# HGRN key and value transposes moved into the local stage, decayed sample states on ScalarE, products by 32-row groups and read-outs in halves

## What is computed

```python
def step(S, inp):
    qc, kc, vc, lf = inp
    G = jnp.cumsum(lf, axis=2)
    Gl = G[:, :, -1]
    o_inter = jnp.einsum('bhik,bhkv->bhiv', qc * jnp.exp(G), S)
    diff = G[:, :, :, None, :] - G[:, :, None, :, :]
    decay = jnp.exp(jnp.where(mask, diff, -jnp.inf))
    A = jnp.einsum('bhik,bhjk,bhijk->bhij', qc, kc, decay)
    o = o_inter + jnp.einsum('bhij,bhjv->bhiv', A, vc)
    S = S * jnp.exp(Gl)[..., None] + jnp.einsum('bhjk,bhjv->bhkv', kc * jnp.exp(Gl[:, :, None, :] - G)[..., None], vc)
    return S, o
```

## Time and profile before

| | |
|---|---|
| median of three timed runs | 2321.52 us |
| the profiled execution | 2320.4 us |
| its span, first to last instruction | 2318.2 us |
| PE / DVE / ACT / POOL busy | 97% / 65% / 55% / 47% |
| mean granted clock of TensorE | 0.984 |
| local_block, layer 0 and layer 1 | 20.18 and 21.73 us |
| hgrn_block, layer 0 and layer 1 | 42.82 and 45.81 us |

### The profile page before, as it was taken

How to read it: one execution, slowest core, us unless ns; L and a number is a source line. 1 busy time by engine, 2 the same in 40 slices (tenths; PEclk the granted TensorE clock), 3 DMA queues, 4 the chain that set the end, 5 groups by cost and what they waited for, 6 DMA issues and landing times. The chain is left out here.

```text
span 2318.2 us, 58007 instructions
## 1 busy us (share of the span) xinstructions
PE 2247.4 (97%) x20562; PEld 2076.7 (90%) x20562; DVE 1495.5 (65%) x3062; ACT 1267.3 (55%) x2437; POOL 1088.8 (47%) x990
## 2 busy tenths in 40 slices
PE   7999999999999999999989999999999999999998
PEld 4967779999998899999978586899999988999997
DVE  3876339943227878788668663598322296887885
ACT  3652225576558855555556422455855596555554
POOL 0221018864446656566304010498444474665661
PEclk8999999999999999999999889999999999999999
DMA  7472135555553389899454702455555534998982
GB/s 290 155 254 94 65 132 182 180 199 185 187 189 137 109 275 312 274 310 314 163 181 160 277 5 102 155 182 181 199 189 185 189 109 139 310 312 272 308 300 100
DMA packets 123816, 455.53 MB, mean 197 GB/s; under 512 B 13745, under 2 KB 14257, under 8 KB 122545
## 3 DMA queue, kind: packets, MB, share of 16 engines
q1 hardware_dynamic: 105264, 386.80, 46.9%
q0 software_dynamic: 18432, 67.12, 10.6%
HBM read 449.37 MB, written 4.49 MB: 196 GB/s over the span
## 5 line engine op out<-in xcount | busy, mean ns | idle before, releaser
L446 POOL TENSOR_TENSOR parts<-ring,parts 128x512 fp32r<-128x512 f32 x358 | 463.4, 1298 | 469.5 <-ACT parts L439 455.7
L439 ACT ACTIVATE parts<-ring 128x512 fp32r<-128x512 f32 x620 | 389.3, 632 | 352.3 <-PE ps_u L493 281.2
L489 PE MATMUL ps_u<-h_parts,parts 128*128 128x256 f32 x4096 | 563.1, 280 | 0.9 <-ACT parts L439 0.6
L2739 PE MATMUL ps_y<-act_parts,parts 128*128 128x256 f32 x4096 | 563.6, 280 | 0.0
L489 PEld LDWEIGHTS ps_u<-h_parts,parts 128*128 128x128 f32 x4096 | 514.7, 188 | 3.2 <-ACT parts L439 1.9
L2739 PEld LDWEIGHTS ps_y<-act_parts,parts 128*128 128x128 f32 x4096 | 515.8, 188 | 0.8 <-ACT parts L2679 0.7
L446 DVE TENSOR_TENSOR parts<-ring,parts 128x512 fp32r<-128x512 f32 x262 | 187.1, 720 | 360.5 <-ACT parts L439 336.1
L2788 POOL TENSOR_TENSOR act_parts<-big,act_parts 128x256 fp32r<-128x256 f32 x256 | 245.0, 957 | 306.2 <-ACT act_parts L2768 306.2
L493 PE MATMUL ps_u<-h_parts,parts 128*128 128x256 f32 x2048 | 322.2, 279 | 1.2 <-DVE parts L446 0.9
L2743 PE MATMUL ps_y<-act_parts,parts 128*128 128x256 f32 x2048 | 322.5, 279 | 0.0
L493 PEld LDWEIGHTS ps_u<-h_parts,parts 128*128 128x128 f32 x2048 | 275.5, 188 | 2.0 <-DVE parts L446 1.3
(11 more groups left out here) (410 smaller groups left out, 2824.5 us busy)
## 6 DMA issues: line engine op xcount, KB each, us to landing
ring<-in_stream SPq DMA_DIRECT2D x506, 512.0 KB, 3.4
more_ring<-in_stream SPq DMA_DIRECT2D x126, 512.0 KB, 3.5
extra_ring<-in_stream SPq DMA_DIRECT2D x32, 512.0 KB, 5.9
mod_ring<-in_stream SPq DMA_DIRECT2D x32, 512.0 KB, 3.3
big<-in_stream SPq DMA_DIRECT2D x16, 512.0 KB, 11.5
out_state_out<-big SPq DMA_DIRECT2D x2, 1440.0 KB, 8.1
big<-in_state SPq DMA_DIRECT2D x2, 1280.0 KB, 10.8
big<-in_mixc SPq DMA_DIRECT2D x2, 1024.0 KB, 8.3
```

The lines of the kernel that those rows point to most:

```text
L439: eng.activation(m.parts[:, q % PARTS, 0, :], half_tile(m, t, half), ACT.Copy).then_inc(s["hi_ready"], 1)
L446: eng.tensor_tensor(m.parts[:, q % PARTS, 1, :], half_tile(m, t, half), m.parts[:, q % PARTS, 0, :].bitcast(F32), ALU.subtract).then_inc(m ...
L489: pe.matmul(out, hi[:, k, :], hr[:, side, kk, 0:tokens], start=(kk + side == 0), stop=False)
L2739: pe.matmul(ps[:, half * KD // 2 + k, :], hi[:, k, :], act_parts[:, j % AHEAD, side, :], start=False, stop=False)
```

## The change

- `ktt` and `vtok` get a place of their own at the end of the area, and the twelve transposes with their six copies move into `local_block`: PE has them in front of 14 fillers in place of 24, then the tiles 4 to 7, and only then the head spread, which now also waits for the copies (`kt_out`).
- In `hgrn_block` the masked values are stored once per row group: the 128 tokens are four groups of 32 rows, each with four chunks of 8. Four masked copies serve 16 chunks. `products(tt, first, end)` runs matmuls over 32 rows each with 256 columns, one bank of `ps_outer` for each row group: 16 matmuls for the first 16 chunks in one call, and 8 in each of two calls for the other 16.
- The samples' decayed states are 16 ScalarE activations of 64 columns in place of two GpSimd products.
- `read_samples` and `read_states` run in halves between the tiles, `sample_products` one pair at a time; the first tile goes ahead of `distance(0)`, `turn(3)` behind the last read-out, and four fillers end PE's list. ScalarE's last copy of rows moves behind the copy of the prompt's last state.
- DVE takes the states in runs of 16, 8 and 8.

The diff, cut to its core:

```diff
-            keep_busy(pe, m, ps[:, 0, :], 24)
+            for tt, (t0, n) in enumerate(TOK):
+                for pair in range(A_PAIRS):
+                    pe.transpose(ps[0:n, tt, pair * P:(pair + 1) * P], m.kt[:, pair, t0:t0 + n], m.ident)
+                for pair in range(A_PAIRS):
+                    mm = pe.transpose(ps[0:n, tt, (2 + pair) * P:(3 + pair) * P], m.zact[:, 4 + pair, t0:t0 + n], m.ident)
+                mm.then_inc(s["turned"], 1)
+            keep_busy(pe, m, ps[:, 3, :], 14)
+            ada(KD // 2, KD)
             pe.wait_ge(s["qk_inverse"], 1)
+            pe.wait_ge(s["kt_out"], 3)
             for n in range(6):
                 mm = pe.matmul(ps[:, n, 0:NT], m.mix("head_spread")[0:12, n * P:(n + 1) * P], norm, start=True, stop=True)
             mm.then_inc(s["qk_spread"], 1)
-            ada(KD // 2, KD)
             turn(0)
...
+            for tt, (_, n) in enumerate(TOK):
+                act.wait_ge(s["turned"], tt + 1)
+                act.activation(flat(m.ktt[0:n, tt, :, :]), ps[0:n, tt, 0:2 * P], ACT.Copy)
+                act.activation(m.vtok[0:n, tt, :], ps[0:n, tt, 2 * P:4 * P], ACT.Copy).then_inc(s["kt_out"], 1)
...
+            def mask_v(tt):
+
+                values = vtok[:, tt, :].rearrange("p (h v) -> p h v", h=4)
+                for j in range(GROUP):
+                    i = act.activation(vm[:, tt, :, j, :], values, ACT.Copy, scale=m.mix("block_rows")[:, j:j + 1])
                 i.then_inc(s["vm_ready"], 1)
 
...
             mask_v(0)
+            mask_v(1)
             copy_rows(act, m, s, ada_rows, ps_mod, 1)
             copy_columns(act, m, s, ps_mod, 1, 1)
-            mask_v(1)
-            mask_v(2)
-            mask_v(3)
+            mask_samples()
+            for pair in range(A_PAIRS):
+                for b in range(NB):
+                    t = NP + NS * b + NS - 1
+                    i = act.activation(m.states[:, pair, 1 + b, :], m.state0[:, pair, b, :], ACT.Copy,
+                                       scale=since[:, pair, t:t + 1])
+                i.then_inc(s[f"kept{pair}"], 1)
             copy_rows(act, m, s, ada_rows, ps_mod, 2)
             copy_columns(act, m, s, ps_mod, 2, 2)
-            mask_v(4)
-            copy_rows(act, m, s, ada_rows, ps_mod, 3)
-            copy_columns(act, m, s, ps_mod, 3, 3)
             for pair in range(A_PAIRS):
                 act.wait_ge(s[f"after{pair}"], BLOCKS)
             act.activation(m.states[:, 0:A_PAIRS, 0, :], after[:, :, BLOCKS - 1, :], ACT.Copy)
-
-        @block.gpsimd
-        def _(pool):
-            for pair in range(A_PAIRS):
-                last = blocks(since, True, NS - 1, NS)[:, pair, :, :].broadcast_to([P, NB, HD])
-                pool.tensor_tensor(m.states[:, pair, 1:, :], m.state0[:, pair, :, :], last, ALU.mult).then_inc(
-                    s[f"kept{pair}"], 1)
+            copy_rows(act, m, s, ada_rows, ps_mod, 3)
+            copy_columns(act, m, s, ps_mod, 3, 3)
...
+            def products(tt, first, end):
+
+                pe.wait_ge(s["vm_ready"], tt + 1)
                 for pair in range(A_PAIRS):
-                    if step >= 2:
-                        pe.wait_ge(s[f"after{pair}"], HALF * (step - 1))
-                    for r in range(2):
-                        rows = slice(r * HD, (r + 1) * HD)
-                        mm = pe.matmul(ps_outer[rows, (2 * step + pair) % 4, :], ktt[:, step // 2, pair, rows],
-                                       vm[:, step % 2, 2 * pair + r, :, :], start=True, stop=True)
-                    mm.then_inc(s["u_ready"], 1)
-
-                pe.wait_ge(s["vm_ready"], 5)
+                    if tt:
+                        pe.wait_ge(s[f"after{pair}"], GROUP * end)
                 for pair in range(A_PAIRS):
-                    pe.wait_ge(s[f"after{pair}"], HALF * 3)
-                    for r in range(2):
-                        rows = slice(r * HD, (r + 1) * HD)
-                        mm = pe.matmul(ps_outer[rows, pair, :], ktt[0:NB * NS, 2, pair, rows],
-                                       vm[0:NB * NS, 0, 2 * pair + r, :, :], start=True, stop=True)
-                    mm.then_inc(s["samples_u"], 1)
-
-            for tt, (t0, n) in enumerate(TOK):
-                for pair in range(A_PAIRS):
-                    pe.transpose(ps_outer[0:n, tt, pair * P:(pair + 1) * P], kt[:, pair, t0:t0 + n], m.ident)
-                for pair in range(A_PAIRS):
-                    mm = pe.transpose(ps_outer[0:n, tt, (2 + pair) * P:(3 + pair) * P], v[:, pair, t0:t0 + n], m.ident)
-                mm.then_inc(s["turned"], 1)
+                    for group in range(first, end):
+                        tokens = slice(32 * group, 32 * group + 32)
+                        for r in range(2):
+                            rows = slice(r * HD, (r + 1) * HD)
+                            mm = pe.matmul(ps_outer[rows, group, pair * GROUP * HD:(pair + 1) * GROUP * HD],
+                                           ktt[tokens, tt, pair, rows], vm[tokens, tt, 2 * pair + r, :, :], start=True, stop=True)
+                mm.then_inc(s["u_ready"], 1)
+
+            def sample_products(pair):
+
+                pe.wait_ge(s["vm_ready"], 3)
+                for other in range(A_PAIRS):
+                    pe.wait_ge(s[f"after{other}"], TB + GROUP * (pair + 1))
+                for r in range(2):
+                    rows = slice(r * HD, (r + 1) * HD)
+                    mm = pe.matmul(ps_outer[rows, pair, :], ktt[0:NB * NS, 2, pair, rows],
+                                   vms[0:NB * NS, 2 * pair + r, :, :], start=True, stop=True)
+                mm.then_inc(s["samples_u"], 1)
+
+            ada(8, 9)
             distance(0)
-            ada(8, 9)
             distance(1)
             ada(9, 11)
             distance(2)
             ada(11, 12)
             distance(3)
-            ada(12, 14)
+            pe.wait_ge(s["sample_free"], 1)
+            read_samples(0, NB // 2)
             distance(4)
+            ada(12, 13)
+            distance(5)
+            products(0, 0, 4)
+            distance(6)
+            ada(13, 14)
+            distance(7)
             ada(14, 16)
-            distance(5)
-            products(0)
-            distance(6)
+            read_samples(NB // 2, NB).then_inc(s["sample_read"], 1)
             turn(1)
-            distance(7)
-            read_samples()
-            ada(16, 20)
-            products(1)
-            ada(20, 24)
-            products(2)
+            ada(16, 17)
+            pe.wait_ge(s["values_done"], 1)
+            read_states(0, 0)
+            ada(17, 19)
+            products(1, 0, 2)
+            read_states(0, 1)
+            ada(19, 21)
+            read_states(1, 0)
+            ada(21, 22)
+            products(1, 2, 4)
+            ada(22, 24)
+            read_states(1, 1)
             turn(2)
-            pe.wait_ge(s["values_done"], 1)
-            read_states(0)
+            sample_products(0)
             ada(24, 27)
-            products(3)
-            read_states(1)
+            read_states(2, 0)
             ada(27, 29)
-            sample_products()
-            ada(29, 32)
-            read_states(2)
+            read_states(2, 1)
+            ada(29, 30)
+            sample_products(1)
+            ada(30, 32)
+            read_states(3, 0)
+            read_states(3, 1).then_inc(s["inter_ready"], 1)
             turn(3)
-            mm = read_states(3)
-            mm.then_inc(s["inter_ready"], 1)
+            keep_busy(pe, m, ps_outer[:, 3, :], 4)
...
-            for turn in range(4):
-                ve.wait_ge(s["u_ready"], 2 * turn + 2)
-                for b in range(turn * HALF, (turn + 1) * HALF):
+            for first, ready in ((0, 1), (TB, 2), (TB + HALF, 3)):
+                ve.wait_ge(s["u_ready"], ready)
+                for b in range(first, TB if ready == 1 else first + HALF):
                     for pair in range(A_PAIRS):
-                        new, j = after[:, pair, b, :], b % HALF
-                        add = ps_outer[:, (2 * turn + pair) % 4, j * HD:(j + 1) * HD]
+                        new = after[:, pair, b, :]
+                        add = ps_outer[:, b // GROUP % 4, (pair * GROUP + b % GROUP) * HD:(pair * GROUP + b % GROUP + 1) * HD]
```

More of the change, by code:

```diff
@@ L1233, in inter, with read_samples @@
                 return pe.matmul(out[rows], state[rows], qt[rows, pair, t:t + n], start=True, stop=True)
[L1235 to L1238 removed]
+            def read_samples(first, end):
+                for b in range(first, end):
                     for pair in range(A_PAIRS):
```

61 lines of the change are left out of this document (25 added, 36 removed).

## The result

| | before | after |
|---|---|---|
| median of the runs | 2318.81 us (18 runs, 2314.68 to 2324.93) | 2335.82 us (18 runs, 2324.51 to 2347.83) |
| ratio after / before, 95% interval | | 1.0077 [1.0064, 1.0089] |
| profiled execution (span) | 2320.4 (2318.2) us | 2347.8 (2345.8) us |
| mean granted clock of it | 0.984 | 0.968 |
| local_block, layer 0 and 1 | 20.18 and 21.73 us | 26.67 and 22.31 us |

The change makes the kernel 17 us slower. The forecast of 2311.0 and its range up to 2320 were both too low; what came is the mechanism of the fourth rival (2333), to which the prediction gave a chance of 0.04. The profiled execution of after is the longest of its 18, so its stages show the effect large: 30.1 us in the two pairs of stages, where the medians differ by 17.0. Its runs scatter over 23 us, those of before over 10.

What follows compares the result with a forecast made beforehand. TensorE, busy 97% of the span, was taken as the bound. Both layers' -11.0 us at full clock and 4.5 back from layer 1 made -15.5; clock falls added 6.1, so -9.4 from 2320.4 gave 2311.0, range 2303 to 2320.

Steps and rivals of the forecast that it cites:

- the fourth rival: HGRN stage: clock stays at half, its dense work of 22 us per layer doubles; 2333 us, chance 0.04.
- The HGRN stage's sum at full clock: HGRN stage, per layer: seven gains and costs on PE sum to -6.0 us.
- first product: HGRN stage start: DVE's 512-column product falls from 1590 ns to 0.70 us with GpSimd silent; gain 1.6 us.
- `distance(0)` at 1.0: HGRN stage start: `distance(0)` starts 1.0 us after the stage in place of 2.63.
- products near 1.1 per call: HGRN stage: overlapping row groups bring the three products calls from 7.8 us to 3.3 together; gain 4.5 us.
- rivals 2 and 3: HGRN stage: 2, row groups don't overlap, 2320, chance 0.13; 3, slow first product isn't GpSimd's doing, 2314, chance 0.10.
- DMA was put at nothing: HGRN stage: tile loads cost nothing, as each tile has six to eight others ahead of it.
- 0.6 for extra changes of kind: HGRN stage: read-outs in halves add changes between kinds of matmul; cost 0.6 us, bounds 0.3 and 1.2.
- the 0.17 at the end: HGRN stage end: `turn(3)` behind the reads and four filler matmuls; net cost 0.17 us.
- the second half of "The clock": HGRN stage, second samples' reads and `turn(1)`: one fall in the two layers, 3.5 us at half, cost 1.7 us.
- The first half: Change from local to HGRN stage: clock falls in both layers; cost 2.2 us per layer, bounds 0 and 3.4.
- The local stage: Local stage, per layer: transposes and tiles ahead of the head spread cost 0.5 us, bounds 0 and 1.3.

Runs made afterwards that it cites:

- three-filler version: Change with three fillers at nine places, old place of tiles 4 to 7, four fillers behind the head spread, three ahead of `distance(0)`: 2310.31 us, 0.9963 of before.
- whole read-outs: Changed kernel with halves of each read-out together again and tiles and sample products ordered as before, product calls further ahead: 2329.56 us, 1.0053 of before.
- extra-work runs: Runs with added useless matmuls; the figures cited are for the changed kernel with six fillers at nine places per layer: 2321.34 us, 1.0015 of before.
- the rounds: Changed kernel with the whole list of product matmuls gone through four times in the first call, twice in the others: 2340.87 us, 1.0102 of before.
- old local order: Changed kernel with tiles 4 to 7 behind the head spread again and 18 fillers in place of 14: 2326.75 us, 1.0041 of before.
- six fillers: Changed kernel with six 256-column bf16 filler matmuls at each of nine places per layer, behind half read-outs and turns: 2321.34 us, 1.0015 of before.
- three fillers with three at the start and the old local order: Changed kernel with three fillers at nine places, three ahead of `distance(0)`, tiles 4 to 7 behind the head spread, no four fillers there: 2308.73 us, 0.9947.
- 128-row bf16 fillers: Changed kernel with whole read-outs, 14 fillers of 512 columns ahead of the first products call, nine of 256 behind each other: 2326.24 us, 1.0026.
- repeats of 32-row fp32 matmuls: Also called whole read-outs with rounds: changed kernel with whole read-outs and the product list repeated four or two times in rounds: 2341.68 us, 1.0081.
- the 26.08 us above: First products call in the changed kernel with each product matmul issued four or two times in a row; that run measured 2405.6 us, 1.0372 of before.

## Why the prediction was wrong, step by step

**The HGRN stage's sum at full clock was right to about half a microsecond.** Stage 36.8 forecast: 36.3 to 36.7 from the three-filler version less its fillers, 36.4 and 36.9 by the cruder reckoning from after. By terms: first product 0.70 forecast, 0.694 measured; `distance(0)` at 1.0, measured 1.01 behind a tile at half clock and 0.88 at full; products near 1.1 per call, measured 1.05 and 1.02; so rivals 2 and 3 are out. DVE's chain and the decayed states hidden, as costed. DMA was put at nothing: no wait in after's HGRN stage, where the half clock gave the tiles time, and none in the three-filler version at full clock; 1.23 us in one layer of the whole read-outs. The 0.6 for extra changes of kind and the 0.17 at the end were not measured apart.

**The step that failed is the second half of "The clock"**, the length and price of the fall behind the samples' second reads: "one fall in the two layers at the price of that at 1310.50, 3.5 us at half, so 1.7". The first half was right in kind: the fall at the change of stage came in both layers (147.5 to 161 with the tile wait in it, 1304.5 to 1311). It was priced at "2.2 per layer", where the prediction's own rows add up to 2.9 in layer 1. For the second fall I took the length from before, where the work behind it brought the clock back. In the new order the work behind it doesn't: it came in both layers, the half clock lasted 44 us in each and cost up to 19 us in each, in the profiled execution, in place of 1.7 us in the two together. The evidence against it, "1314.0 to 1334.4 has a like mixture at 1.00", was weak: that mixture has whole read-outs between runs of two to four tiles and products of 1.9 us on all 128 rows; after's has halves between one to three tiles and products of 1.02 us. The extra-work runs show that it is the clock (54 matmuls more per stage, 14.4 us less in all), and the rounds show that the length of a fall isn't fixed by the code: 43.6 and 63.9 us for the same instructions.

**Rival 4 had the mechanism and nearly the price.** 2333 against a median of 2335.8. Some of that is luck. It doubled only dense work, 22 us per layer, and took two thirds (of 44 in two layers that is 29.3, not the 28.5 written: 2334). The read-outs slow down too (1.03 to 1.81 for 32), so what lay at half in the profiled execution was 38.7 us of the stage, at a cost of up to 19.4 per layer; in the median execution it was less. Its chance of 0.04 was far too small for a change that takes dense work out of a stage in which one layer already fell twice. With the row groups undone 9 us of product time came back and the kernel got no slower, so in this order what the row groups save and what the clock takes for them about cancel.

**The local stage was mis-sized**: 0.5 forecast, bounds 0 to 1.3; measured 6.5 in layer 0 and 0.6 in layer 1 of the profiled execution (2.1 against the 20.18 of full clock, since before's layer 1 had a fall of its own there). The tiles waited for their DMA 2.25 us in layer 0 and 1.55 in layer 1 where the bound had 0.8, and the head spread behind the wait took 2.95 us more at half clock in layer 0 (6.12 for 3.17). The old order gives it back where the clock holds (20.19 / 20.18 in two runs).

**Shares**, from the ratios against after's 1.0077: whole read-outs 0.0024 (5.6 us, not certain), old local order 0.0036 (8.3), both 0.0054 (12.5), row groups undone 0.0018 (4.2, not certain), six fillers 0.0062 (14.4), three fillers with three at the start and the old local order 0.0130 (30). They need not add up to the loss, since each works by the same clock. Which part of the change lets the clock fall, the order of the read-outs, the place of the product calls, their kind or the missing transposes, stays open.

## What to carry to other kernels

In a stage bound by TensorE, look at the granted clock before counting instructions, and give a fall no fixed length: it lasts as long as the work behind it fails to lift it, here 44 us, and then all of PE's work takes nearly twice its time, the sparse matmuls too. When dense matmuls are made shorter or moved away, try the new order together with a few dense fillers at the changes of kind; here three of 256 columns at nine places cost 3.6 us per stage, and with the old local order and three at the start they made the kernel 30 us faster than the change without them, 12 faster than before. A tile load used earlier than before needs its landing time looked up, since a wait there can cost more by the clock than by itself.

## What the runs showed of the hardware

PE's records covered 99% of a stretch and the clock was at half in all of it (43.70 of 44.00 us at 0.50). The Trainium skill (TensorE: Matmul & The Clock Gate, What's actually happening) says that the chip sets the clock by how busy PE has recently been. Taking busy as the share of time that PE's records cover, that rule would have had it at full here, and it wasn't. What the runs show beyond it is that the kind of work counts: at like length, 128-row bf16 fillers gave a ratio of 1.0026 and repeats of 32-row fp32 matmuls 1.0081.

The same instructions can run through a stage at either clock: 743 records in 43.60 us at 0.94 and in 63.86 at 0.61, in one execution. That half clock, by spreading the work out, keeps itself going is a guess that no run tested.

Repeats of a matmul on one tile of the array, issued in a row, took away most of the overlap with the other tiles. Against the 26.08 us above, PE's timeline of whole read-outs with rounds has, at full clock:

```profile
164.78 3.71 PE L1276 MATMUL ps_outer<-big 32*64 32x256 f32 x128
```

That is 0.029 us for a record, against 0.19 at half clock in the other order. Of the factor of 6.6, an estimate gives two to the clock and 3.3 to the order. The Trainium skill (TensorE: Matmul & The Clock Gate, The mechanism) says that matmuls start and end strictly in program order. The slow repeats fit that, as the next tile's matmul doesn't pass the repeat ahead of it, but no run here tests it; in the local stage of before the last record of L1031 starts at 137.40, behind the first of the tile that follows it in the list (L532, 137.16).
